# Peer query: two pieces side by side, key scores three pieces behind, fused steps that pick the indices

## The chip, the cores and the metric

The kernel runs on 1 core of one Trainium2 chip. The metric is the device time of one execution in microseconds. The core has TensorE (PE, with PEld for its weight loads), VectorE (DVE), ScalarE (ACT), GpSimd (POOL) and the DMA queues, one of which (SP) streams the weights.

## The reference

Two transformer blocks over 256 tokens of width 1024, all in float32. The change lies in the last part of the second one, a product-key expert layer (PEER): 8 heads, two halves each, 128 keys per half, and 128 x 128 experts. For each token and head the best 16 keys of each half are taken, then the best 16 of their 256 sums, and those sixteen experts are weighted by a softmax:

```python
q = (hblk @ w_q).reshape(B, TB, PEER_HEADS, 2, PEER_DHALF)
s = jnp.einsum('btphd,phnd->btphn', q, subkeys).astype(jnp.float32)
v, i = lax.top_k(s, PEER_TOPK)
cand = (v[..., 0, :, None] + v[..., 1, None, :]).reshape(B, TB, PEER_HEADS, PEER_TOPK * PEER_TOPK)
cidx = (i[..., 0, :, None] * PEER_NKEYS + i[..., 1, None, :]).reshape(B, TB, PEER_HEADS, PEER_TOPK * PEER_TOPK)
tv, tj = lax.top_k(cand, PEER_TOPK)
eidx = jnp.take_along_axis(cidx, tj, axis=-1)
w = jax.nn.softmax(tv, axis=-1)
```

The gelu of `hblk @ w_down[eidx]`, times `w`, then multiplies `w_up[eidx]`.

## The kernel before

All weights come as a stream of pieces of 128 x 1024, in the order of use, over a ring of three slots. Each piece is split into a high part (ACT copies it to `wh`, line 201) and a low part (ring minus high, to `wl`, line 208, on DVE or, where the code says `low=G`, on POOL). PE multiplies in three products, high x high, high x low, low x high (`mm3`, lines 256 to 258). Three pieces are split ahead (`AHEAD`): the split of piece q + 3 is queued behind the use of piece q. The semaphores `s_high`, `s_low` and `s_used` count pieces. Each engine works off its own instructions in program order, and `Lane.wait` makes it wait for another's count.

The part around the change has four stages. Before it, `rms_operand` norms x, turns it and splits it into `xh` and `xl`, two of the eight column blocks at a time; `need_x(k)` makes PE wait for the block.

The **query stage** (lines 1814 to 1847) takes 16 pieces, one for each head and half (`ph`). `feature_piece` makes a 128 x 256 query in bank `ph % 2` from 24 products, ACT copies it to `qp` (line 1823), PE multiplies it with the keys (line 1831), ACT copies the scores to `sc1`, which has two buffers (line 1835), and DVE takes the best 16 in ten instructions (lines 1840 to 1847). The scores of `ph` are queued on PE behind piece `ph + 1`. ACT's copy of the scores waits for `top[ph - 2]`, which has read the same buffer.

The **lead tiles** (`lead_tile`) follow on PE: 36 pieces of the expert matrix, each 24 products into a bank and a gelu on ACT. PE begins them when all scores are copied (`pe.wait(*copied.values())`). POOL makes the low parts there. Beside them DVE takes the second top 16 (lines 1894 to 1907), turns positions into two index lists (lines 1916 to 1933: the **picking**) and makes the weights (lines 1935 to 1940). For the picking it compares each position with 0 to 15 in a 2048-wide product, multiplies with the indices in a second one and sums over 16, for two lists and two blocks of tokens.

Ahead of lead tile 33 PE turns the two index lists and the weights (`turn_route`, line 1947); it waits for `picked` and `wd` there. Ahead of tile 35 DVE makes the first onehots from them. Then come 64 tiles with the routing products beside them, and the last stage, in loops.

Of the kernel before, what the change touches and what calls it, by code (L numbers as in the profile page):

```python
# [29 lines left out]
ALU = mybir.AluOpType  # L30
ACT = mybir.ActivationFunctionType
AX = mybir.AxisListType
ENG = mybir.EngineType

P = 128
S = 256
NT = S // P
D = 1024
KD = D // P
# [14 lines left out]
PH = 8  # L54
TOPK = 16
# [5 lines left out]
AHEAD = 3  # L61
# [55 lines left out]
def build(nc, a, out):  # L117

    sp = nc.sync
    pe, act = Lane(nc, nc.tensor, "pe"), Lane(nc, nc.scalar, "act")  # L120
    dve, pool = Lane(nc, nc.vector, "dve"), Lane(nc, nc.gpsimd, "pool")
    T, C, V, G = pe.e, act.e, dve.e, pool.e
# [88 lines left out]
    def split(q, i=None, low=V):  # L211
        split_high(q, i)
        split_low(q, i, low)
# [40 lines left out]
    def mm3(o, left, right, start, stop):  # L254

        T.matmul(o, left[0], right[0], start=start, stop=False, skip_group_check=True)  # L256
        T.matmul(o, left[0], right[1], start=False, stop=False, skip_group_check=True)  # L257
        return T.matmul(o, left[1], right[0], start=False, stop=stop, skip_group_check=True)  # L258
# [3 lines left out]
    def need_x(k):  # L262

        if operand["ready"]:
            pe.wait(operand["ready"][k // 2])
# [22 lines left out]
    def feature_piece(dst, low=V):  # L288

        def products(h, l):  # L290
            for k in range(KD):
                need_x(k)
                last = mm3(dst, (h[:, k * P:(k + 1) * P], l[:, k * P:(k + 1) * P]),
                           (xh[:, k, :], xl[:, k, :]), k == 0, k == KD - 1)
            return last
        return step(products, low)
# [1495 lines left out]
    def carve(*shape, dt=F32):  # L1792
        n = int(np.prod(shape))
        v = spare[:, taken_to[0]:taken_to[0] + n]
        taken_to[0] += n
        if dt is not F32:
            v = v.bitcast(dt)
        if len(shape) == 1:
            return v
        letters = "abcde"[:len(shape)]  # L1800
        return v.rearrange(f"p ({' '.join(letters)}) -> p {' '.join(letters)}", **dict(zip(letters, shape)))

    keys = carve(2 * PH, NE)
    ld_keys = load(G, keys, a["subkeys"], "subkeys")
    qp = [carve(S) for i in range(2)]
    sc1 = [carve(NT, NE) for i in range(2)]
    sc2 = [carve(NE) for i in range(2)]
    V16 = carve(NT, 2 * PH, TOPK)
# [1 line left out]
    I16f = carve(NT, 2 * PH, TOPK)  # L1810
    top = {}
    moved, scored, copied = {}, {}, {}
    for st in range(2 * PH + 1):
        ph = st
        if ph < 2 * PH:

            b = bank[ph % 2]
            pe.wait(moved.get(ph - 2))
            if ph == 0:
                G.wait_ge(s_low, pos["q"] + AHEAD)  # L1820
            y = feature_piece(b[:, 0:S], low=G)
            act.wait(y, scored.get(ph - 2))
            moved[ph] = act.did(C.activation(qp[ph % 2], b[:, 0:S], ACT.Copy))
        ph = st - 1
        if ph < 0:
            continue

        pe.wait(moved[ph], ld_keys, copied.get(ph - 2))
        b2 = bank[2 + ph % 2]
        for t in range(NT):  # L1830
            last = T.matmul(b2[:, t * P:(t + 1) * P], qp[ph % 2][:, t * P:(t + 1) * P], keys[:, ph, :],  # L1831
                            start=True, stop=True, skip_group_check=True)
        scored[ph] = pe.did(last)
        act.wait(scored[ph], top.get(ph - 2))
        copied[ph] = act.did(C.activation(sc1[ph % 2], b2[:, 0:S].rearrange("p (t n) -> p t n", t=NT), ACT.Copy))
        dve.wait(copied[ph])
        for t in range(NT):
            s_, r_ = sc1[ph % 2][:, t, :], sc2[t]
            v8, i8 = V16[:, t, ph, :], I16[:, t, ph, :]
            m = dve.did(V.max(v8[:, 0:8], s_))  # L1840
            dve.wait(m)
            V.max_index(i8[:, 0:8], v8[:, 0:8], s_)
            m = dve.did(V.match_replace(r_, v8[:, 0:8], s_, -3.0e38))
            dve.wait(m)
            m = dve.did(V.max(v8[:, 8:16], r_))
            dve.wait(m)
            top[ph] = dve.did(V.max_index(i8[:, 8:16], v8[:, 8:16], r_))
# [35 lines left out]
    TJ = carve(NT, PH, TOPK, dt=U32)  # L1883
    AB = carve(2, NT, PH, TOPK, dt=U32)
    ABf = carve(2, NT, PH, TOPK)
    IJ = carve(2, NT, PH, TOPK)
    Wt = carve(NT, PH, TOPK)
    wsum = carve(NT, PH)
# [29 lines left out]
    dve.wait(m)  # L1918
    m = dve.did(V.tensor_copy(ABf, AB))
    dve.wait(m, ci)  # L1920
    io16 = iota[:, 0:TOPK].unsqueeze(1).broadcast_to([P, PH * TOPK, TOPK])
    c3 = cand.rearrange("p h (a b) -> p (h a) b", a=TOPK)
    for w in range(2):
        for t in range(NT):

            pos_ = ABf[:, w, t, :, :].rearrange("p h k -> p (h k)").unsqueeze(2).broadcast_to([P, PH * TOPK, TOPK])
            idx_ = I16f[:, t, w:2 * PH:2, :].unsqueeze(2).broadcast_to([P, PH, TOPK, TOPK])
            dve.wait((dve.sem, dve.n))
            m = dve.did(V.tensor_tensor(c3, pos_, io16, ALU.is_equal))
            dve.wait(m)  # L1930
            m = dve.did(V.tensor_tensor(c4, c4, idx_, ALU.mult))
            dve.wait(m)
            picked = dve.did(V.tensor_reduce(IJ[:, w, t, :, :], c4, AX.X, ALU.add))
    dve.wait(e_)
    m = dve.did(V.tensor_reduce(wsum, Wt, AX.X, ALU.add))
    dve.wait(m)
# [411 lines left out]
```

## Time and profile before

| | us |
|---|---|
| median of 3 runs | 1883.84 (1882.48 to 1886.82) |
| the profiled execution | 1887.21 |
| its span | 1885.9 |
| PE busy | 1761.1 |
| DVE busy | 1287.3 |
| ACT busy | 901.6 |
| POOL busy | 275.3 |

The span runs from the first to the last instruction on the core. A timeline row has the start in us, the duration in us, engine, line, operation and shapes, and in brackets the idle time of the engine just before it and what ended that. A row of a line's instructions has the count, the shortest, middle and longest duration in ns, and the first and last start. A stretch row has the stretch, its length, the busy time (with the number of instructions) of PE, PEld, DVE, ACT and POOL, the clock granted to PE as a share of full speed, the share of the DMA engines, and GB/s. PE's matmuls are pipelined, so their durations overlap. A row of the waits has who waited for whom, the us in total, how often, and the longest.

### The profile page before, as it was taken

To read this page: it belongs to the slowest core of one execution; us is meant where nothing else is said; L and a number is where in the kernel's file an instruction comes from. 1 tells how busy PE (TensorE), PEld (TensorE's weight loads), DVE (VectorE), ACT (ScalarE), POOL (GpSimd) and SP (SyncE) were. 2 spreads that over 40 slices of the span, in tenths; PEclk is the share of its full clock that TensorE was granted. 3 is DMA by queue.
4 is the path that set the end of the run, shared out by engine and by line. 5 is a ranking of instruction groups with operands and counts; after the bars stand their busy time and mean duration, and the time that the engine had idled before them with its cause. 6 is when DMAs were issued, how large, how long until landed. Compare 5 with 4: busy or idle time off the path is not lost.

```text
span 1885.9 us, 31906 instructions
## 1 busy us (share of the span) xinstructions
PE 1761.1 (93%) x11408; PEld 1579.2 (84%) x11408; DVE 1287.3 (68%) x2255; ACT 901.6 (48%) x1564; POOL 275.3 (15%) x157
## 2 busy tenths in 40 slices
PE   7988999889989998798987998999999999999997
PEld 6757998778869997597777998999999998888885
DVE  4386766776668665856655999677786566666665
ACT  4634443455544433545444444777774444333332
POOL 1022000031121000221112699200000000000000
PEclk9988999899999999898988999999999999999998
DMA  7533856645537665334223454444444555555553
GB/s 256 208 111 124 286 188 242 226 168 172 168 117 244 199 222 170 121 128 134 90 69 128 146 184 144 157 142 139 145 136 161 185 188 178 190 189 188 185 185 121
DMA packets 85893, 317.56 MB, mean 168 GB/s; under 512 B 9568, under 2 KB 9840, under 8 KB 85024
## 3 DMA queue, kind: packets, MB, share of 16 engines
q1 hardware_dynamic: 76464, 278.43, 44.6%
q10 hardware_dynamic: 7776, 26.50, 4.0%
q0 software_dynamic: 1552, 11.25, 1.6%
q8 instruction: 67, 1.10, 0.2%
q14 instruction: 34, 0.28, 0.0%
HBM read 315.08 MB, written 1.05 MB: 168 GB/s over the span
## 4 chain that ended last, share of the span: by engine, by line
PE 57%; DVE 4%; issue 3%; POOL 3%; ACT 2%; DMA 1%; POOLq 0%; DVEq 0%; ACTq 0%; SPq 0%
PE bank L256 17%; PE bank L257 17%; PE bank L258 17%; PE bank L1989 3%; POOL wl L208 2%; DVE wl L208 1%; ACT wh L201 1%; PE bank L346 1%; DMA ring<-in_stream 0%; DMA weighted<-in_subkeys 0%; PE bank L1831 0%; ACT xh L371 0%; PE bank L468 0%; DVE xl L377 0%; PE bank L503 0%
## 5 line engine op out<-in xcount | busy, mean ns | idle before, releaser
L201 ACT ACTIVATE wh<-ring 128x1024 fp32r<-128x1024 f32 x529 | 559.7, 1059 | 796.7 <-PE bank L258 691.3
L208 DVE TENSOR_TENSOR wl<-ring,wh 128x1024 fp32r<-128x1024 f32 x477 | 597.8, 1257 | 472.2 <-ACT wh L201 472.1
L256 PE MATMUL bank<-xh,wh 128*128 128x256 f32 x2072 | 600.6, 290 | 18.9 <-POOL wl L208 7.3
L257 PE MATMUL bank<-xl,wh 128*128 128x256 f32 x2072 | 589.9, 285 | 0.0
L258 PE MATMUL bank<-xh,wl 128*128 128x256 f32 x2072 | 589.4, 284 | 0.0
L256 PEld LDWEIGHTS bank<-xh,wh 128*128 128x128 f32 x2072 | 400.9, 193 | 26.6 <-issue 11.1
L257 PEld LDWEIGHTS bank<-xl,wh 128*128 128x128 f32 x2072 | 401.3, 194 | 1.3
L258 PEld LDWEIGHTS bank<-xh,wl 128*128 128x128 f32 x2072 | 400.8, 193 | 0.0
L256 PE MATMUL bank<-wh,wa_high 128*128 128x512 f32 x512 | 203.2, 397 | 2.3 <-DVE weighted L2008 1.4
L257 PE MATMUL bank<-wl,wa_high 128*128 128x512 f32 x512 | 202.4, 395 | 0.0
L258 PE MATMUL bank<-wh,wa_low 128*128 128x512 f32 x512 | 202.2, 395 | 0.0
L256 PE MATMUL bank<-wh,xh 128*128 128x256 f32 (+1 forms) x400 | 134.4, 336 | 25.6 <-DVE wl L208 10.9
L208 POOL TENSOR_TENSOR wl<-ring,wh 128x1024 fp32r<-128x1024 f32 x52 | 144.0, 2785 | 33.7 <-ACT wh L201 33.6
L257 PE MATMUL bank<-wl,xh 128*128 128x256 f32 (+1 forms) x400 | 130.6, 326 | 0.0
L258 PE MATMUL bank<-wh,xl 128*128 128x256 f32 (+1 forms) x400 | 129.9, 325 | 0.0
L256 PEld LDWEIGHTS bank<-wh,wa_high 128*128 128x128 f32 x512 | 96.3, 188 | 24.9 <-DVE weighted L2008 1.6
L258 PEld LDWEIGHTS bank<-wh,wa_low 128*128 128x128 f32 x512 | 96.2, 188 | 23.4
L257 PEld LDWEIGHTS bank<-wl,wa_high 128*128 128x128 f32 x512 | 96.2, 188 | 22.1 <-issue 0.2
L256 PEld LDWEIGHTS bank<-wh,xh 128*128 128x128 f32 x400 | 79.1, 198 | 37.5 <-DVE wl L208 13.5
L142 POOL DMA_DIRECT2D ring<-in_g_final x1 | 0.6, 573 | 666.5 <-DVE wl L208 666.5
L258 PEld LDWEIGHTS bank<-wh,xl 128*128 128x128 f32 x400 | 79.1, 198 | 5.6
L257 PEld LDWEIGHTS bank<-wl,xh 128*128 128x128 f32 x400 | 79.3, 198 | 5.2 <-issue 0.2
(411 smaller groups left out, 2348.6 us busy)
## 6 DMA issues: line engine op xcount, KB each, us to landing
ring<-in_stream SPq DMA_DIRECT2D x529, 512.0 KB, 3.4
ada<-in_w_ada ACTq DMA_DIRECT2D x48, 512.0 KB, 4.5
rows<-in_rows POOLq DMA_DIRECT2D x1, 2560.0 KB, 10.8
con<-in_early POOLq DMA_DIRECT2D x1, 2078.0 KB, 11.0
rows<-in_rows POOLq DMA_DIRECT2D x2, 1024.0 KB, 5.2
x_feature_major<-in_x_fm ACTq DMA_DIRECT2D x4, 256.0 KB, 7.8
x<-in_x_tm POOLq DMA_DIRECT2D x1, 1024.0 KB, 9.3
weighted<-in_subkeys POOLq DMA_DIRECT2D x1, 1024.0 KB, 7.9
```

Of the source, the lines that this page charges most:

```text
L142: engine.dma_start(dst, src).then_inc(sem, 16)
L201: C.activation(wh[q % AHEAD][:, :], ring[slot][:, :], ACT.Copy).then_inc(s_high, 1)
L208: low.tensor_tensor(wl[q % AHEAD][:, :], ring[slot][:, :], wh[q % AHEAD][:, :], ALU.subtract).then_inc(s_low, 1)
L256: T.matmul(o, left[0], right[0], start=start, stop=False, skip_group_check=True)
L257: T.matmul(o, left[0], right[1], start=False, stop=False, skip_group_check=True)
L258: return T.matmul(o, left[1], right[0], start=False, stop=stop, skip_group_check=True)
L346: last = T.transpose(dst_banks[k // 2][:, (k % 2) * S + t * P:(k % 2) * S + (t + 1) * P], src[:, t, k * P:(k + 1) * P], ident)
L1989: last = T.matmul(bank[g % 4][:, k * P:(k + 1) * P], oh_i[g % 2][:, k, :], oh_j[g % 2][:, k, :], start=True, stop=True, skip_group_check=True)
```

## The change

The first two query pieces are computed together: for each block k of xh and xl PE does the three products of both pieces, in banks 0 and 1. Their splits of the pieces three ahead go to DVE. The scores of `ph` are queued behind piece `ph + 3` instead of `ph + 1`, and `qp` has four buffers. In the picking, 16 fused instructions for each list compare all positions (two blocks of tokens, 256 elements a partition) with n and multiply with the n-th index, each into a slice of `terms`; one sum over the 16 slices follows, with a stride of 1 KB.

```diff
-    qp = [carve(S) for i in range(2)]
+    qp = [carve(S) for i in range(4)]
...
-    for st in range(2 * PH + 1):
+    def feature_pair(dst):
+
+        q = pos["q"]
+        T.wait_ge(s_low, q + 2)
+        for k in range(KD):
+            need_x(k)
+            for i in range(2):
+                h, l = wh[(q + i) % AHEAD], wl[(q + i) % AHEAD]
+                last = mm3(dst[i], (h[:, k * P:(k + 1) * P], l[:, k * P:(k + 1) * P]), (xh[:, k, :], xl[:, k, :]),
+                           k == 0, k == KD - 1)
+                if k == KD - 1:
+                    last.then_inc(s_used, 1)
+        pos["q"] = q + 2
+        split(q + AHEAD)
+        split(q + 1 + AHEAD)
+        return (s_used, q + 2)
+
+    for st in range(2 * PH + 3):
         ph = st
+        if ph == 0:
+            pair_done = feature_pair([bank[0][:, 0:S], bank[1][:, 0:S]])
+        elif 2 <= ph < 2 * PH:
+
+            pe.wait(moved.get(ph - 2))
+            if ph == 2:
+                G.wait_ge(s_low, pos["q"] + AHEAD)
+            y = feature_piece(bank[ph % 2][:, 0:S], low=G)
         if ph < 2 * PH:
-
-            b = bank[ph % 2]
-            pe.wait(moved.get(ph - 2))
-            if ph == 0:
-                G.wait_ge(s_low, pos["q"] + AHEAD)
-            y = feature_piece(b[:, 0:S], low=G)
-            act.wait(y, scored.get(ph - 2))
-            moved[ph] = act.did(C.activation(qp[ph % 2], b[:, 0:S], ACT.Copy))
-        ph = st - 1
+            act.wait(y if ph >= 2 else pair_done, scored.get(ph - 4))
+            moved[ph] = act.did(C.activation(qp[ph % 4], bank[ph % 2][:, 0:S], ACT.Copy))
+        ph = st - 3
         if ph < 0:
             continue
...
-            last = T.matmul(b2[:, t * P:(t + 1) * P], qp[ph % 2][:, t * P:(t + 1) * P], keys[:, ph, :],
+            last = T.matmul(b2[:, t * P:(t + 1) * P], qp[ph % 4][:, t * P:(t + 1) * P], keys[:, ph, :],
...
+    terms = carve(TOPK, NT, PH, TOPK)
...
-    io16 = iota[:, 0:TOPK].unsqueeze(1).broadcast_to([P, PH * TOPK, TOPK])
-    c3 = cand.rearrange("p h (a b) -> p (h a) b", a=TOPK)
     for w in range(2):
-        for t in range(NT):
-
-            pos_ = ABf[:, w, t, :, :].rearrange("p h k -> p (h k)").unsqueeze(2).broadcast_to([P, PH * TOPK, TOPK])
-            idx_ = I16f[:, t, w:2 * PH:2, :].unsqueeze(2).broadcast_to([P, PH, TOPK, TOPK])
-            dve.wait((dve.sem, dve.n))
-            m = dve.did(V.tensor_tensor(c3, pos_, io16, ALU.is_equal))
-            dve.wait(m)
-            m = dve.did(V.tensor_tensor(c4, c4, idx_, ALU.mult))
-            dve.wait(m)
-            picked = dve.did(V.tensor_reduce(IJ[:, w, t, :, :], c4, AX.X, ALU.add))
+        if w:
+            dve.wait(picked)
+        for n in range(TOPK):
+
+            m = dve.did(V.scalar_tensor_tensor(terms[:, n, :, :, :], ABf[:, w, :, :, :], float(n),
+                                               I16f[:, :, w:2 * PH:2, n].unsqueeze(3).broadcast_to([P, NT, PH, TOPK]),
+                                               ALU.is_equal, ALU.mult))
+        dve.wait(m)
+        picked = dve.did(V.tensor_reduce(IJ[:, w, :, :, :], terms.rearrange("p n t h k -> p t h k n"), AX.X, ALU.add))
```

## Rows read from the trace of the kernel before

**Rows 1.** The page, part 1: busy time, share of the span, instructions.
```profile
PE 1761.1 (93%) x11408; PEld 1579.2 (84%) x11408; DVE 1287.3 (68%) x2255; ACT 901.6 (48%) x1564; POOL 275.3 (15%) x157
```
**Rows 2.** Table of stretches; columns as told under the profile above.
```profile
1010.90:1023.00 12.10, 7.79 (x48) 7.17 (x48) 2.84 (x5) 5.21 (x9) 5.34 (x3) 0.86 0.38 129
1023.00:1074.00 51.00, 49.38 (x401) 49.05 (x402) 43.53 (x230) 23.22 (x44) 32.66 (x14) 0.97 0.44 142
...
1130.00:1171.00 41.00, 33.69 (x268) 32.23 (x267) 40.55 (x12) 15.47 (x23) 41.00 (x12) 1.00 0.41 137
...
1192.00:1880.00 688.00, 678.43 (x4237) 606.92 (x4235) 472.77 (x769) 350.88 (x692) 1.99 (x3) 1.00 0.50 166
...
1023.10:1026.30 3.20, 3.20 (x15) 3.20 (x16) 1.41 (x8) 0.38 (x1) 0.00 (x0) 0.50 0.50 168
```
**Rows 3.** Timeline of POOL, low parts of the lead tiles.
```profile
1125.77 2.40 POOL L208 TENSOR_TENSOR wl<-ring,wh 128x1024 fp32r<-128x1024 f32 x1 [0.46 <-ACT wh L201]
1128.65 49.35 POOL L208 TENSOR_TENSOR wl<-ring,wh 128x1024 fp32r<-128x1024 f32 x14 [0.48 <-ACT wh L201]
```
**Rows 4.** Timeline of PE, query stage to lead tile 33.
```profile
1018.84 0.28 PE L258 MATMUL bank<-xh,wl 128*128 128x256 f32 x1
1023.07 1.20 PE L1831 MATMUL bank<-weighted 128*128 128x128 f32 x4 [3.95 <-DMA weighted<-in_subkeys]
...
1031.29 0.60 PE L1831 MATMUL bank<-weighted 128*128 128x128 f32 x4
...
1073.92 0.36 PE L256 MATMUL bank<-xh,wh 128*128 128x256 f32 x1 [0.52 <-ACT weighted L1835]
...
1180.28 0.36 PE L256 MATMUL bank<-xh,wh 128*128 128x256 f32 x1
```
**Rows 5.** Waits between 1130 and 1180.
```profile
PE bank L256 <- POOL wl L208: 7.3, 7, 1.3
```
**Rows 6.** Timeline of DVE, start of the picking.
```profile
1128.49 2.29 DVE L1929 TENSOR_TENSOR weighted<-weighted,keep 128x2048 f32<-128x2048 f32 x1
1130.81 4.38 DVE L1931 TENSOR_TENSOR weighted<-weighted 128x2048 f32<-128x2048 f32 x1
1135.22 2.29 DVE L1933 TENSOR_REDUCE weighted<-weighted 128x128 f32<-128x2048 f32 x1
```
**Rows 7.** Timelines of DVE and ACT, last xl pair and the first two pieces.
```profile
1013.65 0.69 DVE L377 TENSOR_TENSOR xl<-rms_tmp,xh 128x512 fp32r<-128x512 f32 x1 [0.42 <-ACT xh L371]
...
1016.33 1.06 ACT L201 ACTIVATE wh<-ring 128x1024 fp32r<-128x1024 f32 x1 [2.72 <-PE bank L258]
1017.30 0.37 ACT L1823 ACTIVATE weighted<-bank 128x256 f32<-128x256 f32 x1
```
**Rows 8.** Timeline of DVE, first instruction of the top 16 of four heads.
```profile
1024.79 0.29 DVE L1840 MAX8 weighted<-weighted 128x8 f32<-128x128 f32 x1 [10.45 <-ACT weighted L1835]
...
1033.18 0.30 DVE L1840 MAX8 weighted<-weighted 128x8 f32<-128x128 f32 x1
...
1072.94 0.29 DVE L1840 MAX8 weighted<-weighted 128x8 f32<-128x128 f32 x1
...
1076.10 0.27 DVE L1840 MAX8 weighted<-weighted 128x8 f32<-128x128 f32 x1
```
**Rows 9.** Timelines of DVE and POOL at 760, and the instructions of line 1940.
```profile
760.25 0.17 DVE L1178 SCALAR_TENSOR_TENSOR gains<-mod,vec 128x8 f32<-128x8 f32 x1
760.34 2.38 DVE L1179 SCALAR_TENSOR_TENSOR gains<-mod,vec 128x8 f32<-128x8 f32 x1
...
760.27 2.42 POOL L431 TENSOR_TENSOR x<-z,rows 128x1024 f32<-128x1024 f32 x1 [9.67 <-DVE mod L1176]
...
L1940 DVE TENSOR_TENSOR weighted<-weighted x2: 1736/2113/2490, 1174.0 to 1175.7; 128x128 f32<-128x128 f32 x2
```
**Rows 10.** Instructions of lines 2081 and 1381.
```profile
L2081 DVE TENSOR_TENSOR weighted<-weighted,gelu x28: 416/419/420, 1437.0 to 1589.7; 128x256 f32 x24, 128x256 f32<-128x256 f32 x4
...
L1381 DVE TENSOR_TENSOR win<-shifted,vec x8: 344/354/366, 844.0 to 864.3; 128x120 f32<-128x120 f32 x8
```

## The prediction

> **What bounds the kernel now.** I read the page's busy shares first: TensorE (PE) is busy 93% of the 1885.9 us span, so the question is where the rest goes [rows 1]. The table of stretches answers it for the part that the change touches: PE misses 4.3 of 12.1 us in 1010.9 to 1023, 1.6 of 51 in the query stage and 7.3 of 41 in 1130 to 1171; after 1192 it is busy 678 of 688 us [rows 2]. So whatever moves PE at 1180 moves the end by as much. The clock column of the stretch right behind an idle PE reads 0.50 (1.2 GHz), with 15 products in 3.2 us [rows 2]; at the pace of the tiles, 24 products in 2.88 us [rows 3], they would take 1.6 us less.
>
> The single timelines then name the waits. At 1018.84 PE issues the last product of its second piece and then sits until 1023.07 for the subkeys' DMA, 3.95 us. At the end of the query stage it waits for the last copied score (0.52 us), and the lead tiles begin at 1073.92 [rows 4]. From 1130 it waits for POOL's low parts, 7.3 us in 7 waits [rows 5]; each restart also loses the overlap of a product (0.28 us long, the next 0.12 us behind), so it is some 8 to 9 us.
>
> The last loss is the port that VectorE (DVE) and POOL share. Beside a POOL subtract the 2048-wide products of the picking take 4.38 us, alone 2.29; the sums always 2.29 [rows 6]. In the same time 14 of POOL's subtracts take 49.35 us, 3.53 each, where one alone takes 2.40 and PE asks for one per 2.88 [rows 3]. A DVE instruction with two SBUF inputs and a POOL instruction take turns: the later one waits for the whole of the other.
>
> **The change part by part.** *Two pieces side by side.* The xl pairs still arrive up to 1014.34 [rows 7], but each now feeds 12 products instead of 6. If the clock is granted as now (0.86 over 1010.9 to 1023 [rows 2]), 48 products end at about 1018.2, where the second piece now ends near 1019 [rows 4]. Then a new wait: piece 2 writes bank 0 again, and ACT reaches the copy out of bank 0 only after the two wh copies that `feature_pair` has queued before it, 0.97 us apart [rows 7]: 1018.0 + 2 x 0.97 + 0.36 = 1020.3. PE stalls 2.1 us. The lows of these two pieces go from POOL to DVE, which is idle there (10.45 us before 1024.79 [rows 8]), so they cost nothing; POOL's own lows begin one piece later and are needed three pieces later.
>
> *Scores three pieces behind.* Pieces 2 and 3 end at 1020.3 + 2 x 2.88 = 1026.1, after the keys have landed, so the 3.95 us wait is gone. Score 0 then follows piece 3. In the steady state DVE starts a head's top 16 1.89 us after the piece ends (1031.29 to 1033.18 [rows 4, 8]), so now at 1028.0. Here the gain stops: what PE must wait for at the end is not its own work. `copied[15]` reuses the buffer that `top[13]` reads, and PE starts the lead tiles only after it. DVE starts head k at 1028.0 + 3.31 k, as PE feeds it, up to k = 12 (1067.7); the last three are free of PE but cost DVE 3.16 us each (1072.94 to 1076.10 [rows 8]). `top[13]` is done at 1067.7 + 6.3 = 1074.0, the copy and its semaphores 0.55 later: lead tiles from 1074.6 instead of 1073.92, **+0.6 us**. PE, finished with its own share near 1068, idles 6 us there, and the slow clock behind it stays (1.6 us now, about 1.5 then). The stage's 4 us are thus not shortened but moved. The top 16 end at 1080.4 instead of 1079.3, and the 49.2 us of the second top 16 between there and the picking [rows 6, 8] are untouched, so the picking starts at 1129.6. Bounds: if the bank wait is smaller by its 2.1 us, all this is 2 us earlier; if the stall brings a slow clock, as the one at 1018.84 did, 1.2 us later.
>
> *The picking.* It removes 8 products of 2048 (33 us, since all but the first wait) and 4 sums of 2.29, and adds 32 fused steps of 256 elements and 2 sums of 4096. Alone a 256-wide two-input step takes 0.42 us [rows 10], and neighbours overlap by 0.08, so 0.34 each: 32 cost 10.9 us. But the fused step has two SBUF inputs too, and the trace shows this very operation beside POOL: 0.17 us before POOL's instruction started, 2.38 us for the next one with as few elements, released when POOL's ended [rows 9]. So the number of *instructions* counts, not of elements. How many get through for each POOL subtract? POOL rests 0.48 us between two (waiting for ACT) [rows 3]. The waiting step runs at once (0.27 us); the second issues about 0.20 us after POOL's end, inside the gap, and holds POOL back until 0.61; a third would issue at 0.54, when POOL is already in line, and POOL goes first, as it does between two neighbouring products at the end of the routing weights (1.74 and 2.49 us for 128 elements [rows 9]). PE's pace leaves 2.88 - 2.40 = 0.48 us per subtract for this, and 0.27 + 0.34 f = 0.48 gives f = 0.6: **1.6 steps per 2.88 us, 1.78 us each**. Bounds: 1 per subtract (2.88) and 2 (1.44). PE is no longer starved, for POOL is only held back by what it has in hand.
>
> A sum of 4096 costs 4.4 us at the rate of the present one [rows 6]. But it reads with a stride of 1 KB. The only strided SBUF read of DVE in the trace, 120 elements 64 bytes apart, takes 0.354 us; by the contiguous row (0.419 for 256, of which 0.267 for the elements at the sums' rate) it would be 0.277 [rows 10]. That is 0.65 ns more per element and makes the sum 7.1 us. I take 7.1, the nearer row in its access, and keep 4.4. The Trainium skill (SBUF — State Buffer, Door 1: The DMA port swizzle) has a rule against this: elements of 4 bytes on separate 16-byte lines do not get full bandwidth. Read as half the rate it would make the sum 8.7 us and the total below 1.9 us worse. The one strided row agrees in sign; a stride of 1 KB has no row here.
>
> *The sum.* PE reaches the turning of the routes at 1074.6 + 33 x 2.88 + 1.5 = 1171.1 instead of just before 1180.28 [rows 4]. DVE: 16 steps from 1129.6 to 1158.1, sum to 1165.2. PE now waits, POOL works off what is released (ACT 1.06, POOL 2.40) until 1174.9, and 9.7 / 1.78 = 5.4 steps get through; the other 10.6 go free at 0.34 until 1178.5, the sum until 1185.6. Then the sum, reciprocal and two products of the weights, none over 256 wide, 1.4 us by [rows 10] (an estimate), and the last transposes: tile 33 starts at 1187.3, where it now starts at 1180.28 [rows 4]. That is +7.0, and PE comes out of 14 us of idling at 1.2 GHz, which cost 1.6 us each time above: **+8.6 us**. With the cheap sums the same steps give +5.4. The wait covers what it hides: DVE's onehots after it find POOL idle and are not later. What is late next is nothing: after 1192 PE is the bound.
>
> The profiled run of before is 1887.21 us, its span 1885.9, the median of three runs 1883.84. I add the difference to the median: **1892.4 us**.
>
> **The rivals.** *The fused step does not contend* (A, 0.17). Then both rounds take 2 x (5.4 + 7.1) = 25 us, done at 1155, PE arrives unstarved at 1171.1 and does not wait: tile 33 at 1171.7, -8.6 us, **1875**. Against it stands [rows 9]; for it that the steps seen there have 8 elements. If three steps pass per subtract (POOL's gap longer than 0.54 us), DVE is in time as well, but POOL is held 0.47 us longer per tile and gives half back: 1880.
>
> *One step per subtract* (B, 0.12), if POOL is always ready when it ends, as it was in 1130 to 1178 [rows 3]. Then 16 steps need until 1175, the rest runs free: tile 33 at 1196.5, **1902**; with cheap sums 1896. Against it: small steps leave POOL ahead of PE, so it does rest.
>
> *The two delays cancel* (C, 0.18): the query stage starts 2 us earlier, two steps per subtract, cheap sums, and one POOL wait fewer in the 49.2 us. Each is worth 2 us: **1880 to 1887**. The dividing point is when the last fused step ends: for no change it must be by 1172.
>
> **How the numbers follow.** The forecast has 0.53 (1887 to 1896 with its bounds), A 0.17, B 0.12, C 0.18. 0.2%, about what can be told here from no change, is 3.8 us: faster below 1880.1, slower above 1887.6. A gives faster 0.17 and C 0.03 of it; C gives most of same; the forecast, with 0.03 below the line, and B give slower. Range 1879 to 1900: it leaves out the first form of A (0.14) and the upper part of B (0.06).
>
> **What would show it.** Right: fused steps of 0.4 us in groups with one of about 2.4 between; POOL near 2.4 to 3.0 each with no starved PE before 1171; a PE wait of over 8 us ahead of the transposes; sums of over 4.4 us; a PE wait of some 2 us after the pair and of 6 before the lead tiles. Wrong: fused steps all near 0.4 us, PE reaching the transposes later than the last sum, or lead tiles starting near 1069.

## The result, and the profile after

The changed kernel takes 1894.79 us, the median of 7 runs, beside 1885.51 us for the kernel before in 7 runs next to them: a ratio of 1.0052 with a 95% interval of 1.0035 to 1.0069, so 6.6 to 13.0 us slower, 9.8 in the middle. The profiled execution took 1897.49 us, its span is 1896.2.

The first part of the page (busy time, share of the span, instructions), against [rows 1]:

```profile
PE 1766.0 (93%) x11408; PEld 1585.4 (84%) x11408; DVE 1292.2 (68%) x2279; ACT 901.5 (48%) x1564; POOL 256.0 (14%) x155
```

PE has the same 11408 products. POOL is 19 us less busy, yet the span is 10.3 us longer. Not all of that is the change's. The keys' load, which POOL issues after the last xl piece, starts the stage in both kernels. It is issued 2.9 us later in this execution than in the one of before, and the last xl pair, which the change doesn't touch, is later by the same (1016.54 against 1013.65 [rows 7]). From the issue to the last instruction it is 7.4 us longer (878.3 against 870.9). POOL's timeline, first of the kernel before, then of the changed one (start, us, engine, line, operation, idle time before it):

```profile
1014.99 0.63 POOL L142 DMA_DIRECT2D weighted<-in_subkeys  x1 [10.02 <-DVE xl L377]
```

```profile
1017.89 0.63 POOL L142 DMA_DIRECT2D weighted<-in_subkeys  x1 [10.02 <-DVE xl L377]
```

So from here on times are counted from this issue, and written "issue + n". PE's timeline of the changed kernel, as [rows 4] of the one before:

```profile
1021.90 0.39 PE L256 MATMUL bank<-xh,wh 128*128 128x256 f32 x1 [2.09 <-ACT weighted L1842]
...
1070.91 1.16 PE L1850 MATMUL bank<-weighted 128*128 128x128 f32 x8 [0.86 <-ACT weighted L1854]
...
1077.84 0.55 PE L256 MATMUL bank<-xh,wh 128*128 128x256 f32 x1 [5.77 <-ACT weighted L1854]
...
1187.09 1.83 PE L1964 MATMUL bank<-keep,weighted 128*128 128x128 f32 x6 [11.28 <-DVE weighted L1950]
1188.58 0.56 PE L256 MATMUL bank<-xh,wh 128*128 128x256 f32 x1
...
1193.59 0.28 PE L256 MATMUL bank<-xh,wh 128*128 128x256 f32 x1
```

The wait for the keys is gone. In its place stand 2.09 us for the copy out of bank 0 and 5.77 us for the last copied score. The lead tiles begin at issue + 59.95, where they began at issue + 58.93. Then PE waits 11.28 us for the picking, and tile 33 begins at issue + 170.69, against issue + 165.29 before [rows 4]: 5.4 us later.

The table of stretches, columns as before, read against [rows 2]:

```profile
1021.90:1025.10 3.20, 3.20 (x17) 3.20 (x18) 1.19 (x2) 0.22 (x1) 0.00 (x0) 0.61 0.72 246
...
1077.90:1081.10 3.20, 3.20 (x15) 3.20 (x16) 2.99 (x17) 0.00 (x0) 0.00 (x0) 0.50 0.00 0
1081.10:1084.30 3.20, 3.20 (x18) 3.20 (x17) 2.96 (x14) 0.91 (x1) 0.00 (x0) 0.54 0.00 0
1130.00:1171.00 41.00, 41.00 (x344) 41.00 (x344) 40.93 (x26) 20.83 (x31) 35.82 (x15) 1.00 0.55 184
...
1188.60:1193.20 4.60, 4.60 (x23) 4.60 (x22) 2.50 (x4) 0.41 (x2) 0.00 (x0) 0.50 0.00 0
```

Between 1130 and 1171 PE lacks nothing now (41.00 of 41.00, where it had 33.69). What that gave, and more, it loses elsewhere. After each of the three waits the granted clock falls to 0.50, that is 1.2 GHz: after the 2.09 us it averages 0.61 over 3.2 us, after the 5.77 us it stays low for 6.2 us (the 0.54 is some 0.25 us of full speed at the end of that stretch), after the 11.28 us for 4.6. What the last two cost is less than half of their length, since a product lies 0.21 us behind the one before it there, and 0.12 at the full clock. The way from the first lead tile to the transposes takes 97.97 us (1077.84 to 1175.81), where it takes 95.66 behind a clock of 1.00 (four score buffers, below): 2.3 us. And tile 33 takes 5.01 us until tile 34 begins (1188.58 to 1193.59), where it took 2.94 in the kernel before (1180.28 [rows 4] to 1183.22): 2.1 us. PE's timeline of the kernel before there:

```profile
1183.22 0.28 PE L256 MATMUL bank<-xh,wh 128*128 128x256 f32 x1
```

DVE's timeline of the picking, as [rows 6], and POOL's beside it:

```profile
1125.37 2.50 DVE L1937 TENSOR_SCALAR weighted<-weighted 128x256 uint32<-128x256 uint32 x1
1127.90 0.43 DVE L1939 CAST weighted<-weighted 128x512 f32<-128x512 uint32 x1
1128.37 23.02 DVE L1946 SCALAR_TENSOR_TENSOR weighted<-weighted 128x256 f32<-128x256 f32 x16
1151.42 7.68 DVE L1950 TENSOR_REDUCE weighted<-weighted 128x256 f32<-128x4096 f32 x1
1159.14 20.86 DVE L1946 SCALAR_TENSOR_TENSOR weighted<-weighted 128x256 f32<-128x256 f32 x16
1180.03 7.00 DVE L1950 TENSOR_REDUCE weighted<-weighted 128x256 f32<-128x4096 f32 x1
```

```profile
1136.67 2.57 POOL L208 TENSOR_TENSOR wl<-ring,wh 128x1024 fp32r<-128x1024 f32 x1 [0.32 <-ACT wh L201]
...
1156.84 2.40 POOL L208 TENSOR_TENSOR wl<-ring,wh 128x1024 fp32r<-128x1024 f32 x1 [0.46 <-ACT wh L201]
...
1177.04 2.34 POOL L208 TENSOR_TENSOR wl<-ring,wh 128x1024 fp32r<-128x1024 f32 x1 [0.49 <-ACT wh L201]
1195.01 2.40 POOL L208 TENSOR_TENSOR wl<-ring,wh 128x1024 fp32r<-128x1024 f32 x1 [15.62 <-ACT wh L201]
```

The first 16 steps take 23.02 us, which is 8 times POOL's period of 2.88 us: two steps for each subtract. Taken one by one they alternate, a step that waits for the subtract and one that runs through:

```profile
1130.80 0.41 DVE L1946 SCALAR_TENSOR_TENSOR weighted<-weighted 128x256 f32<-128x256 f32 x1
1131.14 2.62 DVE L1946 SCALAR_TENSOR_TENSOR weighted<-weighted 128x256 f32<-128x256 f32 x1
```

The second 16 meet seven subtracts, the last one ending at 1179.4, and the second sum ends only at 1187.0. POOL's rows grow by 0.17 us beside the first 16 steps (2.57 against 2.40), and its rest shrinks by as much; beside the second 16 it is 0.06 or less. So POOL is held up a little, and never so long that PE misses a low part.

The instructions of the step (shortest, median and longest in ns, first and last start):

```profile
L1946 DVE SCALAR_TENSOR_TENSOR weighted<-weighted x32: 410/423/2632, 1128.4 to 1179.6; 128x256 f32<-128x256 f32 x32
```

### The profile page after: what moved, and what is told of

It is laid out like the page before. It is cut to its first block, busy times and chain, and to the rows that moved or that the text cites. A ratio compares the mean times of both kernels' runs of the same rounds, so it can differ in the third digit from the quotient of the medians.

```text
span 1896.2 us, 31941 instructions
## 1 busy us (share of the span) xinstructions
PE 1766.0 (93%) x11408; PEld 1585.4 (84%) x11408; DVE 1292.2 (68%) x2279; ACT 901.5 (48%) x1564; POOL 256.0 (14%) x155
## 3 DMA queue, kind: packets, MB, share of 16 engines
HBM read 315.08 MB, written 1.05 MB: 167 GB/s over the span
## 4 chain that ended last, share of the span: by engine, by line
PE 57%; DVE 10%; ACT 2%; issue 1%; POOL 0%; DMA 0%; ACTq 0%; DVEq 0%; POOLq 0%; SPq 0%
PE bank L256 17%; PE bank L257 17%; PE bank L258 17%; PE bank L2006 3%; DVE weighted L1946 2%; DVE wl L208 1%; ACT wh L201 1%; DVE weighted L1950 1%; PE bank L346 1%; DVE weighted L1927 0%; DVE weighted L1922 0%; DVE weighted L1925 0%; DVE weighted L1923 0%; PE bank L468 0%; DVE weighted L1920 0%
## 5 line engine op out<-in xcount | busy, mean ns | idle before, releaser
L208 POOL TENSOR_TENSOR wl<-ring,wh 128x1024 fp32r<-128x1024 f32 x50 | 124.7, 2500 | 59.9 <-ACT wh L201 59.9
## 6 DMA issues: line engine op xcount, KB each, us to landing
rows<-in_rows POOLq DMA_DIRECT2D x1, 2560.0 KB, 10.6
```

The source lines that it names most:

```text
L208: low.tensor_tensor(wl[q % AHEAD][:, :], ring[slot][:, :], wh[q % AHEAD][:, :], ALU.subtract).then_inc(s_low, 1)
```

## The experiments

The theory: the fused steps lose the port to POOL by count of instructions, and this is nearly all of the slowdown, since the query's gain is given back ahead of the lead tiles. The main rivals: the steps would run as fast without POOL's subtracts in the way (Q), the query stage does gain (R), and the strided sum is what costs.

### One part of the change alone

The query stage of the changed kernel with the picking of the one before (in short):

```
-    for st in range(2 * PH + 1):            # the old query stage
+    pair_done = feature_pair(...)           # the new one, scores three pieces behind
     (picking as before: two products of 2048 and a sum, eight times)
```

> The query stage of the change with the picking of before. Theory (the query part only moves its idle time, because the lead tiles wait for the copy that waits for the top 16 of head 13): PE waits about 2 us after the pair and 5 to 6 us ahead of the lead tiles, these start 0.5 to 1.5 us later than before, measured from the last xl pair; the time is -1 to +2 us against before, which is no change. Rival R (the query part gains its 4 us, and the picking of the change eats them and more): 4 us faster than before, lead tiles 4 us earlier.

Measured: 1889.17 us, 1.0014 [1.0000, 1.0028], some 2.6 us slower than before (0 to 5.3). PE's timeline, first lead tile and tile 33:

```profile
1072.60 0.55 PE L256 MATMUL bank<-xh,wh 128*128 128x256 f32 x1 [5.78 <-ACT weighted L1854]
...
1180.01 0.36 PE L256 MATMUL bank<-xh,wh 128*128 128x256 f32 x1
```

With its keys issued at 1012.64 the lead tiles begin at issue + 59.96, as in the change itself. Rival R is refuted: the wait for the keys left and 2.1 and 5.8 us of other waits came. POOL still starves PE for 7.2 us between 1120 and 1180, as the old products do. In the middle it cost a little more than the theory's upper bound of 2; the interval holds that bound.

The other part: the new picking on the old query stage.

```
     (query stage as before, scores one piece behind)
+            m = dve.did(V.scalar_tensor_tensor(terms[:, n, :, :, :], ABf[:, w, :, :, :], float(n), ...
```

> The query stage of before with the fused picking of the change. Theory: all of the slowdown is here; two fused steps for each subtract of POOL, about 23 us for 16 of them, PE waits 10 to 13 us ahead of the transposes: 6 to 10 us slower than before. Rival R: 12 to 14 us slower than before, the 4 us that the query part gave back missing.

Measured: 1888.89 us, 1.0016 [1.0000, 1.0032], about 3 us slower (0 to 6.0). That misses the 6 to 10 expected, and with it the theory that all of the slowdown is here. The mechanism was there, as the timelines show: two steps per subtract in the first 16 and PE waiting 12.62 us for the sum. But the stage in front of it was different, though its code is that of the kernel before. DVE, then PE:

```profile
1123.92 23.16 DVE L1927 SCALAR_TENSOR_TENSOR weighted<-weighted 128x256 f32<-128x256 f32 x16
...
1154.84 16.78 DVE L1927 SCALAR_TENSOR_TENSOR weighted<-weighted 128x256 f32<-128x256 f32 x16
```

```profile
1021.12 0.68 PE L1831 MATMUL bank<-weighted 128*128 128x128 f32 x4 [1.05 <-DMA weighted<-in_subkeys]
...
1070.46 0.36 PE L256 MATMUL bank<-xh,wh 128*128 128x256 f32 x1 [0.52 <-ACT weighted L1835]
...
1178.72 1.83 PE L1945 MATMUL bank<-keep,weighted 128*128 128x128 f32 x6 [12.62 <-DVE weighted L1931]
1180.20 0.56 PE L256 MATMUL bank<-xh,wh 128*128 128x256 f32 x1
```

Issued at 1015.93, the keys landed in 5.1 us, where they took 7.9 before. PE waited 1.05 us for them instead of 3.95 [rows 4], and the clock in the 3.2 us behind was 1.00 where it had been 0.50 [rows 2]. So the lead tiles came at issue + 54.53, 4.4 us earlier: 2.9 of the wait and some 1.6 of the slow clock. With them PE reached its wait earlier, POOL ran dry earlier, and the second 16 steps took 16.78 us instead of 20.86. That leaves two questions: is the slow landing of the keys an accident of one execution, and does an earlier start of the lead tiles by itself shorten the picking?

### The landing of the keys in the kernel before

The unchanged kernel was profiled twice more.

> The kernel before, for a second profile of its query stage. Theory (its first profile shows an unusually late landing of the keys, 7.9 us after the issue): keys 5 to 6 us after the issue, PE waits 1 to 2.3 us for them, lead tiles about 56 us after the start of the last xl pair's subtract, where the first profile has 60.3. Rival: 7.9 us again, and 60 us.

> The kernel before once more. Theory: keys 5 to 6 us after the issue, lead tiles about 56 us after the last xl pair. Rival: 7.9 us and 60 us.

Measured: 1891.16 and 1890.46 us in one run each. The issues of the keys' load, with size and median time to landing, in the first of the two:

```profile
weighted<-in_subkeys POOLq DMA_DIRECT2D x1, 1024.0 KB, 7.6
```

PE waited 3.62 us for it, and 4.20 us in the other run, where it took 7.6 us as well; the lead tiles began at issue + 58.56 and + 59.50. So the slow landing is no accident of one execution: all three of the kernel before have it. In the change and the nine variants the same load took 5.1 to 6.1 us, those with the old query stage among them (5.1 and 5.4). Its issue, size and surroundings look alike in the trace. A stretch from the issue on, of the kernel before (6 us) and of the new picking alone (5 us), shows where the difference lies:

```profile
1014.99:1020.99 6.00, 4.13 (x30) 3.93 (x29) 0.00 (x0) 2.66 (x4) 3.64 (x3) 0.90 0.52 171
```

```profile
1015.93:1020.93 5.00, 4.14 (x30) 3.93 (x29) 0.00 (x0) 2.10 (x3) 3.00 (x2) 0.88 0.62 213
```

171 GB/s over 6 us are 1.03 MB, 213 over 5 us 1.07 MB, all queues together. So by these rates all but some 4% of the load has moved in the kernel before as well, and the rest comes late, when the next piece of the weights is on its way. Why it does stays open.

### The lead tiles earlier, the picking untouched

Four buffers instead of two for the copied scores. The copy of score 15 then need not wait for the top 16 of head 13.

```
-    sc1 = [carve(NT, NE) for i in range(2)]
+    sc1 = [carve(NT, NE) for i in range(4)]
-        act.wait(scored[ph], top.get(ph - 2))
+        act.wait(scored[ph], top.get(ph - 4))
```

> The change with four score buffers and nothing else, so that the fused steps still take turns with POOL. Theory (the end of the picking is set by when PE stops feeding POOL): the lead tiles start 5 us earlier, PE still waits 11 to 14 us at the transposes, but POOL runs dry 5 us earlier too and more steps go free: the picking ends 5 to 6 us earlier, counted from the last xl pair, and the time is 4 to 7 us below the change. Rival (PE waits for the picking anyway): an earlier PE only waits longer, and the time is within 2 us of the change.

Measured: 1888.31 us in 12 runs, 1.0020 [1.0010, 1.0031], some 6 us less than the change. PE, then DVE:

```profile
1068.02 0.36 PE L256 MATMUL bank<-xh,wh 128*128 128x256 f32 x1 [0.52 <-ACT weighted L1854]
...
1177.58 1.83 PE L1964 MATMUL bank<-keep,weighted 128*128 128x128 f32 x6 [13.90 <-DVE weighted L1950]
```

```profile
1127.26 23.16 DVE L1946 SCALAR_TENSOR_TENSOR weighted<-weighted 128x256 f32<-128x256 f32 x16
...
1158.16 12.33 DVE L1946 SCALAR_TENSOR_TENSOR weighted<-weighted 128x256 f32<-128x256 f32 x16
1170.52 7.00 DVE L1950 TENSOR_REDUCE weighted<-weighted 128x256 f32<-128x4096 f32 x1
```

And the stretch behind the start of the lead tiles in the table of stretches:

```profile
1068.00:1071.20 3.20, 3.18 (x26) 3.20 (x27) 2.99 (x17) 0.00 (x0) 0.18 (x1) 1.00 0.50 165
```

The keys were issued at 1013.33, so the lead tiles come at issue + 54.69, 5.3 us earlier, and the clock behind them is at 1.00, where it was at 0.50. PE arrives at the transposes at issue + 150.35 (1177.58 - 13.90), 7.6 us earlier than in the change (1187.09 - 11.28, issue + 157.92). The end is 6 us earlier, although PE waits 2.6 us longer for the picking, and although the picking begins 3.4 us later after the issue (+ 113.93 against + 110.48, as three of DVE's instructions ahead of it met a subtract and not one). That is the loop to see here: an earlier PE stops feeding POOL earlier, POOL leaves the port, and the rest of the steps run freely (the second 16 in 12.33 us instead of 20.86).

Do the two parts of the change add? The times alone can't tell: 2.6 (0 to 5.3) and 3 us (0 to 6.0) against 9.8 (6.6 to 13.0) together. The traces, one execution each, say that they don't. Tile 33 begins at issue + 167.37 with the new query stage alone and at + 164.27 with the new picking alone, where the three profiles of the kernel before have + 164.73 to + 165.29 and the change + 170.69. With the slow clock behind tile 33 (1.9 us with the new picking alone, 2.1 in the change) that is 2 to 3 us and about 1 us for the parts, and 7.5 to 8 for both. The loop gives a reason: beside the new picking alone PE arrived at the transposes at issue + 150.17 (1178.72 - 12.62), so the new query stage brings it there 7.8 us later, and as in this run most of such a shift reaches the end.

### The port

The positions that the steps compare, in PSUM instead of SBUF, so that a step has one SBUF input:

```
-    ABf = carve(2, NT, PH, TOPK)
+    ABf = bank[0].rearrange("p (w t h k) -> p w t h k", w=2, t=NT, h=PH)
```

> The change with the positions (ABf) kept in PSUM bank 0, which is free there, so that each fused step has one SBUF input only; nothing else is different. Theory (the port that DVE and POOL share is the cost): steps of 0.4 us without waits, 16 in under 6 us, sums of 7 to 7.7 us as before, POOL back to 2.40 us, PE does not wait at the transposes: 7 to 10 us faster than before, 16 to 19 faster than the change. Rival Q (32 instructions and strided sums are too slow on their own, port or not): steps stay above 1 us each, PE still waits for picked, and the time is within 4 us of the change.

Measured: 1880.23 us, 0.9964 [0.9954, 0.9975], 4.7 to 8.7 us faster than before (6.8 in the middle, just short of the 7 expected) and some 16 faster than the change. The instructions of the step, then DVE's timeline, then POOL's:

```profile
L1946 DVE SCALAR_TENSOR_TENSOR weighted<-bank,weighted x32: 414/415/424, 1122.9 to 1141.0; 128x256 f32<-128x256 f32 x32
```

```profile
1122.90 5.39 DVE L1946 SCALAR_TENSOR_TENSOR weighted<-bank,weighted 128x256 f32<-128x256 f32 x16
1128.33 7.71 DVE L1950 TENSOR_REDUCE weighted<-weighted 128x256 f32<-128x4096 f32 x1
```

```profile
1124.94 2.41 POOL L208 TENSOR_TENSOR wl<-ring,wh 128x1024 fp32r<-128x1024 f32 x1 [0.46 <-ACT wh L201]
```

The longest step is 424 ns, where it was 2632. 16 of them take 5.39 us beside the same subtracts, POOL's rows are back at 2.41, and there is no wait ahead of the transposes. Rival Q is refuted: not the steps are slow, but their second SBUF input beside POOL's. The Trainium skill says so (SBUF — State Buffer, Who interferes with whom): a DVE instruction with two SBUF inputs contends with a GpSimd instruction that reads SBUF, one with at most one SBUF input, outside DVE's 2-port perf modes, doesn't. The trace agrees, with 1.44 us a step against 0.34. One input alone is no safeguard: the TENSOR_SCALAR at 1125.37 in the change has a single SBUF input and takes 2.50 us, where its neighbour of the same shape takes 0.29. Which mode it ran in no row shows.

Next, whether the price goes by instructions or by elements: the same elements in twice as many steps of half the size.

```
+            for t in range(NT):
+                m = dve.did(V.scalar_tensor_tensor(terms[:, n, t, :, :], ABf[:, w, t, :, :], float(n), ...
```

> The change with each fused step cut into two of 128 elements, 64 in all: the same elements, twice the instructions. Theory (a step is let through while POOL pauses 0.48 us, and what counts is how many start in that pause): 3 or 4 of the half steps for each POOL subtract of 2.88 us, so 32 of them take 23 to 31 us instead of 23, and the time is 0 to 10 us above the change. If only the number of instructions counted, 2 per subtract, 32 would take 46 us. If the elements counted, 32 would take 11 to 12 us.

Measured: 1898.71 us in one run. DVE's timeline:

```profile
1128.22 28.57 DVE L1947 SCALAR_TENSOR_TENSOR weighted<-weighted 128x128 f32<-128x128 f32 x32
```

```profile
1133.74 2.49 DVE L1947 SCALAR_TENSOR_TENSOR weighted<-weighted 128x128 f32<-128x128 f32 x1
...
1136.56 0.28 DVE L1947 SCALAR_TENSOR_TENSOR weighted<-weighted 128x128 f32<-128x128 f32 x1
1136.76 2.49 DVE L1947 SCALAR_TENSOR_TENSOR weighted<-weighted 128x128 f32<-128x128 f32 x1
```

32 half steps take 28.57 us, 3.2 of them per subtract. A price by the instruction alone, at 1.44 us, would make it 46 us, one by elements 11 to 12. So it is neither. Taken one by one, a half step of 2.4 to 2.5 us is followed by two or three of 0.28, 0.2 apart, where a whole step is followed by one: what counts is how many steps fit between one subtract and the next, the first having waited at the port and the others as long as they issue before POOL is ready.

### The sum

The steps write with a stride, so that the sum reads densely:

```
-    terms = carve(TOPK, NT, PH, TOPK)
+    terms = carve(NT, PH, TOPK, TOPK)       # written as terms[:, :, :, :, n], summed as it lies
```

> The change with terms laid out so that the sum over the 16 slices reads neighbouring elements, and the fused steps write with a stride of 64 bytes instead. Theory (the long sums come from the stride): sums of 4.4 us instead of 7.7 and 7.0, steps still two per POOL subtract, the picking done 3 to 6 us earlier and the time 3 to 6 us below the change. Rival (a strided write costs as much as a strided read): steps hold the port 0.17 us longer, one per subtract instead of two at times, and the time is not below the change.

Measured: 1894.73 us, 1.0051 [1.0032, 1.0070], the change's own ratio. DVE's timeline, and the instructions of the step:

```profile
1124.07 31.42 DVE L1946 SCALAR_TENSOR_TENSOR weighted<-weighted 128x256 f32<-128x256 f32 x16
1155.53 4.42 DVE L1950 TENSOR_REDUCE weighted<-weighted 128x256 f32<-128x4096 f32 x1
```

```profile
L1946 DVE SCALAR_TENSOR_TENSOR weighted<-weighted x32: 571/1894/2837, 1124.1 to 1177.9; 128x256 f32<-128x256 f32 x32
```

The sum is 4.42 us, as the rate of the old ones gave it, so the stride of the reading is what makes it 7.0 to 7.7. The total did not follow, the theory's 3 to 6 us failed, and the rival is what came: a strided write makes the step 0.571 us (0.415 dense), only 1.5 fit per subtract, and what the two sums saved (14.68 - 8.84 = 5.8 us) the steps took (31.42 + 18.50 instead of 23.02 + 20.86, 6.0 us).

### What is left when both are mended

Positions in PSUM and four score buffers:

> The positions in PSUM, and four score buffers (sc1) instead of two, so that the copy of head 15 no longer waits for the top 16 of head 13. Theory (the query part's gain ends in that wait): the 5.8 us wait ahead of the lead tiles is gone, and the slow clock behind it; 5 to 8 us faster than with the positions in PSUM alone, 11 to 14 faster than before. Rival (something else holds the lead tiles, or DVE is late for the transposes instead): within 2 us of the positions in PSUM alone.

Measured: 1870.16 us, 0.9917 [0.9901, 0.9934], 15.6 us faster than before, slightly more than expected; beyond the PSUM edit alone it is 0.0047, 8.9 us, of which the timeline shows 5.3 as an earlier start of the lead tiles:

```profile
1069.39 0.36 PE L256 MATMUL bank<-xh,wh 128*128 128x256 f32 x1 [0.52 <-ACT weighted L1854]
```

The keys were issued at 1014.69, so this is issue + 54.70; it was + 59.95 with the PSUM edit alone. Now the old query stage with the new picking in PSUM:

> The query stage of before with the fused picking and the positions in PSUM. Theory (the query part as made costs time, the more so when the keys land in 5 us and not in 8): lead tiles 4 to 5 us earlier, counted from the last xl pair, than with the change's query stage; 3 to 6 us faster than the positions in PSUM with the change's query stage, 9 to 12 faster than before. Rival (the query part gains): slower than that by 2 us or more.

Measured: 1872.05 us, 0.9936 [0.9916, 0.9956], 12 us faster than before and about 5 faster than the new query stage with the same picking (0.9964). The lead tiles begin at issue + 54.91 (issued at 1011.98), without the wait of 5.8 us:

```profile
1066.89 0.36 PE L256 MATMUL bank<-xh,wh 128*128 128x256 f32 x1 [0.52 <-ACT weighted L1835]
```

So, as the change has it, its new query stage is worth less than the old one (the two intervals just touch; tile 33, counted from the issue, is 6.2 us earlier, at + 152.07 against + 158.27); with four score buffers the two can't be told apart (0.9917 and 0.9936, overlapping intervals).

Last, the copies out of the banks ahead of the two wh copies that `feature_pair` queues on ACT (in short):

```
-        split(q + AHEAD)                    # both, in feature_pair
-        split(q + 1 + AHEAD)
+        if ph == 1:                         # behind the copy of piece 1
+            split(pos["q"] - 2 + AHEAD)
+            split(pos["q"] - 1 + AHEAD)
```

> The same as with four score buffers, and ACT copies the first two queries out of their banks ahead of the two wh copies instead of behind them. Theory: the 2.1 us wait of piece 2 shrinks to under 0.8, and 1 to 3 us go with it against the four score buffers alone. Rival: the splits come late instead, PE waits for the low part of piece 3 as long, and nothing changes.

Measured: 1869.04 us, 0.9910 [0.9893, 0.9928]. The waits of the query stage (engine, line, what it waited for: us in total, times, longest):

```profile
PE bank L256 <- ACT weighted L1840: 0.6, 1, 0.6
```

The bank wait fell from 2.1 to 0.6 us, as the order of ACT's queue said, and the lead tiles begin at issue + 51.67 instead of + 54.70. In the total the 1.1 us against the version without it are within the intervals, so the times don't show that gain. This is the fastest version measured, some 17 us faster than the kernel before and 26 faster than the change.

## Why the prediction held, and where its terms were off

The forecast was +8.6 us. Tile 33 came 5.4 us later after the keys' issue, against 7.0 forecast, and the slow clock behind it cost 2.1, against 1.6: together 7.5, which is what the profiled spans differ by behind the issue (7.4). The interval of the timed 9.8 (6.6 to 13.0) holds both sums. The 5.4 is counted from 165.29 in the first profile of the kernel before; the other two have 164.89 and 164.73, which would make it up to 6.0. The mechanism came as told: the steps take turns with POOL, PE idles ahead of the transposes, and the query stage gives its gain back. That the sum came out so near owes something to luck, since terms missed by several microseconds and cancelled.

- **The pair and the bank wait**: 2.1 us forecast, 2.09 in the timeline, and the run with the copies moved ahead shows the two wh copies as its cause.
- **No gain from the query stage**: the lead tiles were forecast 0.6 us later with 6 us of idling ahead of them; they came 1.0 later than in the first profile of before (0.4 to 1.4 over its three), after 5.77 us. The bound that a slow clock follows the stall, 1.2 us later, is what came: 0.61 behind the 2.09 us. That `top[13]` holds `copied[15]` is shown: with four buffers the wait falls to 0.52 us.
- **The keys**: the step took their landing as given. It was 7.6 to 7.9 us in the kernel before and 5.1 to 6.1 in every changed one, with the old query stage too. With the faster landing the old stage waits 1.05 and 2.32 us for them and not 3.95, so part of what the new stage avoids goes without it. The step stayed right because the end of the stage hung on DVE.
- **Start of the picking**: forecast 1129.6 in the time of before; 1128.37 less the 2.9 us is 1125.5, 4 us early. The 49.2 us of the second top 16 were carried over with the three port waits in them that stood in the kernel before; here only one instruction met POOL (2.50 us). Which of DVE's small instructions meet a subtract changes with every shift (three again with the new picking alone), so these 4 us are luck.
- **Steps per subtract**, the mis-sized term: 1.6 forecast, 2.0 measured, which was the stated bound. The step let the second instruction hold POOL back until 0.61 us after the end of the subtract before. POOL's rows (2.57 long after a rest of 0.31) say 0.48: it issues at 0.20 and holds the port for the time of its elements, 0.27, and not for the 0.34 that two neighbours lie apart. 0.48 is just what PE's pace leaves.
- **The free steps**: 10.6 were forecast to run free behind PE's arrival, and about two did. With two steps per subtract and an earlier start DVE needed less; PE came later. It reached the transposes at 1175.8 (1172.9 in the time of before, 1171.1 forecast). Of the 1.8 us the clock behind the lead tiles' start is 0.8: the slow stretch was carried over at 1.5 us of cost, and 6.2 us of it cost 2.3. The lead tiles' own start gives 0.3, and their pace the rest (95.66 us at the full clock, and not 33 x 2.88 = 95.04). POOL's end in the working, 1174.9, is 0.3 us later than its own terms make it (1171.1 + 1.06 + 2.40).
- **The sums**: 7.1 us forecast, 7.68 and 7.00 measured. Dense it is 4.42, so the stride costs 2.6 to 3.3 us. The Trainium skill's rule on lines of 16 bytes (SBUF — State Buffer, Door 1: The DMA port swizzle), read as half the rate, gave an estimate of 8.7, 4.3 us of them for the stride: it had the sign right, and reading it as half was too much.
- **The end**: PE waited 11.28 us and not 14. The errors had both signs: the start 4 us early and the denser steps shortened DVE's way, the missing free steps and the longer sum gave most of it back.

Of the rivals, A (no contention) is what the PSUM run makes true: 6.8 us faster (4.7 to 8.7) where A was priced at 8.6; the slow clock behind the lead tiles' start, 1.5 us in the working, is under 1 us of the difference. B (one step per subtract) shows in no run; the dense sum with its longer steps came nearest, with 1.5. C needed two steps per subtract, one POOL wait fewer in the second top 16, an earlier query stage and cheap sums. The first came, and of the second more than asked (two waits fewer); the other two didn't, and PE still waited 11.28 us.

## What to carry to other kernels

Beside an engine that shares a read port, count the small instructions that fit between two of its large ones; if the loop hangs on that, put one of their two inputs into PSUM, which here made a step four times cheaper without another edit. A wait that is removed at the front of a pipelined stage gives nothing while the stage's last buffer is released by another engine: look first for the buffer that the last step reuses (here two carved buffers more were worth 6 to 9 us). And don't count on adding the prices of two parts when one of them sets how long the other is in contention.

## What the runs showed of the hardware that was not expected

- A strided sum of 4096 elements that needs no second input is still a tenth slower while POOL and PE are at work (7.68 to 7.71 us against 7.00 once both wait). Dense it is 4.42 us in either case. Which of the two engines it is no run separates.
- Instructions with one SBUF input can wait for POOL too: the cast of 512 elements ahead of the picking takes 2.57 us in the kernel before and 0.43 in the change, and 0.69 into PSUM while a subtract runs.
- A two-input step of the change that waits for the port lasts up to 2.63 us, but the steps delay POOL by at most 0.19 us per subtract: the two sides do not pay the same.
- Writing 256 elements 64 bytes apart costs 0.571 us instead of 0.415, so moving a stride from the reader to 16 writers saved nothing.
- The same load of 1024 KB lands in 7.6 to 7.9 us in the kernel before and in 5.1 to 6.1 in the ten others, two of them with the same code around it. All but some 4% has moved 6 us after the issue in the kernel before too; no run here says why the rest is late.
- The wait of 0.52 us ahead of the lead tiles is the same in six programs. The clock falls to 0.50 for some 3 us behind it in two of the three profiles of the kernel before and with the old query stage and PSUM, and stays at 1.00 in the third profile of the kernel before, with the new picking alone and in the three programs with four score buffers. So one and the same program shows both; what decides was not found. The stretch behind it in that third profile:

```profile
1076.28:1079.48 3.20, 3.20 (x27) 3.20 (x28) 3.00 (x17) 0.00 (x0) 0.88 (x1) 1.00 0.44 161
```

- A PE that waits longer for a chain on DVE can finish earlier: 13.90 us of waiting with the end 6 us sooner than with 11.28, because the wait itself takes POOL off the port.
